# Second feed-forward of a two-block kernel: the up product of four slots in eight as seven block products, in 13 of 16 passes

## The chip, the cores and the metric

The kernel runs on one core of a Trainium2 chip. The metric is the device time of one execution in microseconds (us). Three executions of the kernel before took 2435.14, 2436.72 and 2437.55 us; the median is 2436.72 us.

## The reference, cut to what matters

Two transformer blocks of width 2048 run over 256 tokens in float32. The change lies in the last step of the second block, whose hidden width is 8192:

```
D_MODEL, SEQ = 2048, 256
D_FF_2 = 4 * D_MODEL

u = rms_norm_2(h, norm_mlp_w[l])
h = h + jnp.square(jax.nn.relu(u @ w_up[l])) @ w_down[l]
...
return rms_norm_2(h, norm_final_w)
```

## The kernel before, in words

All large products have one form. A **slot** is a piece of a weight matrix of 256 rows and 512 columns, 512 KB, held as [128, 2 x 512]. The chip's SyncE (SP) issues one DMA for each slot into one of four places of `raw` (`RING = 4`), ScalarE (ACT) rounds it to fp32r in `w_hi` (`split`, L904 to L910), VectorE (DVE) writes what is left over to `w_lo` = `raw` - `w_hi` (L1422 to L1426), and TensorE (PE) multiplies: for each of 2 token tiles and 2 row tiles three matmuls of 512 moving columns (`gemm`, L484 to L500: activation high x weight high, activation high x weight low, activation low x weight high), 12 in all. The activations are the stationary operand, so each matmul loads 128x128 of them.

The ring sets the order: the load of slot q starts when `w_lo` of slot q-4 is done (L401, L442, semaphore `w_lo_ready`); ACT splits slot q three slots ahead of PE, as soon as the load has landed and PE has done slot q-4 (`landed`, `slot_done`); DVE follows ACT (`w_hi_ready`); PE waits for `w_lo_ready`. Every engine works its queue in the written order.

The second feed-forward runs in 16 passes over chunks of 512 hidden columns. A pass i has 16 slots: 0 to 7 are the up product of chunk i over 2048 input rows (`ups2`; operands `B_hi`, `B_lo`; PSUM banks 0 and 1), 8 to 15 the down product of chunk i-1 into four column chunks of the result (`downs2`, operands `C_hi`, `C_lo`, banks `D2_BANKS`, two slots for each chunk), which DVE adds to `resid` (`add_chunk`, L1473). After slot 7 ACT takes the up product out of PSUM in four pieces with the rms scale and a relu (L933), DVE squares it (L1923) and transposes it in 32x32 blocks (L1926), and GpSimd (POOL) sends it to DRAM and back in four DMAs (`turn_rows`, L2131 and L2135), which completes the transposition. In the next pass ACT and DVE split what came back into `C_hi` and `C_lo` (`up2_operand`, L1348 and L1909, behind the split of slot 5). POOL does nothing else in this stage.

## Time and profile before

| | |
|---|---|
| median of three executions | 2436.72 us |
| the profiled execution, span | 2435.7 us |
| PE matmul busy | 2409.6 us, 99% |
| DVE busy | 1642.3 us, 67% |
| ACT busy | 1285.9 us, 53% |
| POOL busy | 215.8 us, 9% |
| one pass of the second feed-forward | 41.4 us |

The span is the time from the first to the last instruction on the core; about 1 us lies around it. A matmul's record lasts from its issue to its modelled end, so records overlap: the pace of PE is the distance between two starts, not the mean of a record. A line number can be that of a helper that serves the whole kernel (L496 to L498 are all of the matmuls of `gemm`).

### The profile page before, as it was taken

What the parts mean: (1) busy time and instruction counts of PE and PEld (TensorE: products, weight loads), DVE (VectorE), ACT (ScalarE), POOL (GpSimd) and SP (SyncE); (2) the same over time, 40 slices, a digit from 0 to 9 for tenths busy, and PEclk for the clock granted to TensorE, in tenths of its full rate; (3) what the DMA queues carried; (4) which work ended last, traced back from release to release, by engine and by line L of the source; (5) the groups of instructions that cost most, each with busy time, mean ns of one, the idle gap of its engine ahead of it and who ended that gap; (6) DMA issues with size and microseconds to landing.
All of it is one profiled execution on the core that took longest, in us unless ns stands there. A gap on an engine that the chain in (4) does not pass through costs nothing. (4 is left out here: it accounts for less than half of the span.)

```text
span 2435.7 us, 32600 instructions
## 1 busy us (share of the span) xinstructions
PE 2409.6 (99%) x11468; PEld 2111.4 (87%) x11468; DVE 1642.3 (67%) x1831; ACT 1285.9 (53%) x1715; POOL 215.8 (9%) x364
## 2 busy tenths in 40 slices
PE   8999999999999999999999999999999999999997
PEld 7888888888888888888889888888888888888886
DVE  5666665777777777776877655566666666666666
ACT  6555555655555555564444555555554444444444
POOL 0111101100000000000010100000110000000000
PEclk9999999999999999999999999999999999999999
DMA  7877777887787778767566866578877877777775
GB/s 233 274 216 225 216 218 233 248 239 234 240 236 238 235 234 237 221 195 227 179 200 189 245 193 209 178 226 252 250 235 216 235 224 230 227 231 226 224 232 161
DMA packets 270391, 545.79 MB, mean 224 GB/s; under 512 B 22011, under 2 KB 23395, under 8 KB 270179
## 3 DMA queue, kind: packets, MB, share of 16 engines
q1 hardware_dynamic: 244064, 469.82, 63.4%
q0 software_dynamic: 22192, 70.28, 10.4%
q10 hardware_dynamic: 4051, 4.59, 0.6%
q8 instruction: 50, 0.82, 0.1%
q14 instruction: 34, 0.28, 0.0%
HBM read 508.93 MB, written 35.68 MB: 224 GB/s over the span
## 5 line engine op out<-in xcount | busy, mean ns | idle before, releaser
L1426 DVE TENSOR_TENSOR w_lo<-raw,w_hi 128x1024 fp32r<-128x1024 f32 x887 | 1078.9, 1222 | 661.6 <-ACT w_hi L910 656.5
L910 ACT ACTIVATE w_hi<-raw 128x1024 fp32r<-128x1024 f32 x887 | 934.3, 1056 | 919.0 <-PE acc L498 785.1
L496 PE MATMUL acc<-w_hi,A_hi 128*128 128x512 f32 x1932 | 741.2, 384 | 2.2 <-DVE A_lo L1909 1.7
L498 PE MATMUL acc<-w_hi,A_lo 128*128 128x512 f32 x1932 | 733.2, 379 | 0.0
L497 PE MATMUL acc<-w_lo,A_hi 128*128 128x512 f32 x1932 | 733.1, 379 | 0.0
L496 PEld LDWEIGHTS acc<-w_hi,A_hi 128*128 128x128 f32 x1932 | 366.0, 189 | 55.2 <-issue 2.9
L498 PEld LDWEIGHTS acc<-w_hi,A_lo 128*128 128x128 f32 x1932 | 365.9, 189 | 51.0
L497 PEld LDWEIGHTS acc<-w_lo,A_hi 128*128 128x128 f32 x1932 | 366.2, 190 | 49.3
L496 PE MATMUL acc<-w_hi,B_hi 128*128 128x512 f32 x800 | 304.9, 381 | 0.6 <-DVE B_lo L1693 0.6
L496 PE MATMUL acc<-w_hi,C_hi 128*128 128x512 f32 x800 | 303.7, 380 | 0.0
L497 PE MATMUL acc<-w_lo,B_hi 128*128 128x512 f32 x800 | 303.6, 379 | 0.0
L498 PE MATMUL acc<-w_hi,C_lo 128*128 128x512 f32 x800 | 303.6, 379 | 0.0
L497 PE MATMUL acc<-w_lo,C_hi 128*128 128x512 f32 x800 | 303.5, 379 | 0.0
L498 PE MATMUL acc<-w_hi,B_lo 128*128 128x512 f32 x800 | 303.5, 379 | 0.0
L496 PEld LDWEIGHTS acc<-w_hi,B_hi 128*128 128x128 f32 x800 | 151.6, 189 | 22.0 <-DVE B_lo L1693 1.0
L496 PEld LDWEIGHTS acc<-w_hi,C_hi 128*128 128x128 f32 x800 | 151.5, 189 | 21.3 <-DVE w_lo L1426 0.2
L498 PEld LDWEIGHTS acc<-w_hi,B_lo 128*128 128x128 f32 x800 | 151.5, 189 | 21.2
L498 PEld LDWEIGHTS acc<-w_hi,C_lo 128*128 128x128 f32 x800 | 151.5, 189 | 21.2
L497 PEld LDWEIGHTS acc<-w_lo,C_hi 128*128 128x128 f32 x800 | 151.5, 189 | 21.1
L497 PEld LDWEIGHTS acc<-w_lo,B_hi 128*128 128x128 f32 x800 | 151.5, 189 | 20.9
L1473 DVE TENSOR_TENSOR resid<-resid,acc 128x1024 f32<-128x1024 f32 x114 | 138.7, 1217 | 9.5 <-PE acc L498 9.0
L933 ACT ACTIVATE scratch<-acc,small 128x256 f32<-128x256 f32 x196 | 77.1, 473 | 64.4 <-PE acc L498 64.4
(208 smaller groups left out, 1296.5 us busy)
## 6 DMA issues: line engine op xcount, KB each, us to landing
raw<-in_up SPq DMA_DIRECT2D x304, 512.0 KB, 4.5
raw<-in_w SPq DMA_DIRECT2D x271, 512.0 KB, 4.4
raw<-in_down SPq DMA_DIRECT2D x216, 512.0 KB, 4.9
raw<-in_wo SPq DMA_DIRECT2D x64, 512.0 KB, 4.9
turn_rows<-scratch POOLq DMA_DIRECT2D x23, 512.0 KB, 3.2
scratch<-turn_rows POOLq DMA_DIRECT2D x92, 128.0 KB, 5.8
up_rows<-scratch POOLq DMA_DIRECT2D x21, 512.0 KB, 5.2
scratch<-up_rows POOLq DMA_DIRECT2D x84, 128.0 KB, 5.1
```

The source lines that it names most:

```text
L496: pe.matmul(o, hi[:, kt, ts], wh, start=first and kk == 0, stop=False)
L497: pe.matmul(o, hi[:, kt, ts], wl, start=False, stop=False)
L498: m = pe.matmul(o, lo[:, kt, ts], wh, start=False, stop=last and kk == SLOT_K - 1)
L910: act.activation(w_hi[:, q % RING, :], raw[:, q % RING, :], ACT.Copy).then_inc(w_hi_ready, 1)
L933: m = act.activation(by_block(dst, t)[:, h * JT // 2:(h + 1) * JT // 2], src, func, scale=scale[:, t:t + 1])
L1426: dve.tensor_tensor(w_lo[:, q % RING, :], raw[:, q % RING, :], f32(w_hi[:, q % RING, :]), ALU.subtract).then_inc(w_lo_ready, 1)
L1473: dve.tensor_tensor(v, v, acc[:, banks[0]:banks[1] + 1, :].rearrange("p t (n h) -> p t h n", h=2), ALU.add).then_inc(done, 1)
```

## The change

In passes 2 to 14 (13 passes) the up slots 1, 3, 5 and 7 are multiplied by Strassen's scheme in Winograd's form. A slot's product is seen as a 2x2 block product (two token tiles by two row tiles, times two row tiles by two halves of 256 columns) and takes seven block products of 256 columns, each as three matmuls, so 21 matmuls of 256 columns (`gemm_by_seven`). Four of the seven use sums of weight blocks. POOL makes them from `raw` in three instructions per slot (`make_sums`, two chained waits between them), and ACT and DVE split these sums in addition to 768 of the slot's own 1024 columns. The sums go into free room of `A_hi` and `A_lo`. Four sums of activation blocks for all four slots are made once, ahead of pass 2 (`make_forms` on POOL, ACT and DVE). The other up slots of these passes keep their 12 matmuls of 512 columns, but with the columns in another order (`gemm_by_halves`: each half of 256 for itself).

The seven products gather in PSUM banks 0 to 3. Behind slot 7 ACT copies banks 2 and 3 to SBUF, DVE combines them in three small instructions and adds banks 0 and 1 to the result (`quarters`); ACT applies the relu to it in four pieces and then squares it, which DVE did before. These relu and square stand behind two down slots (`q == 1`), the transposition on DVE behind three (`q == 2`), and `up2_operand` stands behind the split of slot 7 instead of slot 5. The down product uses banks 4 to 7 in turn in place of six banks and waits for the additions of the chunk two before.

```diff
-        D2_BANKS, D2_LAST = [BK[1], BK[2], BK[3], BK[1]], [BK[0], BK[2], BK[3], BK[1]]
+        D2_BANKS, D2_LAST = [BK[2], BK[3], BK[2], BK[3]], [BK[0], BK[2], BK[3], BK[1]]
...
+        Q = CW // 2
+        SEVEN = (1, 3, 5, 7)
+        SEVEN_FROM, SEVEN_TO = 2, FFN2 - 1
...
+            def gemm_by_halves(R, p, hi, lo, kp, banks, first):
+
+                pe.wait_ge(w_lo_ready, RING * R + p + 1)
+                ring = p % RING
+                for t in range(TT):
+                    for kk in range(SLOT_K):
+                        kt = kp * SLOT_K + kk
+                        wh, wl = (half_in_turn(w[:, ring, kk * CW:(kk + 1) * CW]) for w in (w_hi, w_lo))
+                        o, ts = half_columns(acc[:, banks[t], :]), slice(t * P, (t + 1) * P)
+                        pe.matmul(o, hi[:, kt, ts], wh, start=first and kk == 0, stop=False)
+                        pe.matmul(o, hi[:, kt, ts], wl, start=False, stop=False)
+                        m = pe.matmul(o, lo[:, kt, ts], wh, start=False, stop=False)
...
+                for bank, half, act_pair, w_pair, starts, stops in (
+                        (x0, 1, of_token(1, 0), of_slot(3), False, False),
+                        (x0, 0, of_form(3), of_slot(2), False, True),
+                        (c1, 1, of_token(0, 0), of_slot(1), True, False),
+                        (x1, 1, of_token(1, 1), of_sum(3), False, True),
+                        (c0, 0, of_form(0), of_sum(0), True, False),
+                        (c1, 0, of_form(1), of_sum(2), False, True),
+                        (c0, 1, of_form(2), of_sum(1), False, True)):
+                    o = columns(acc[:, bank, half * Q:(half + 1) * Q])
+                    wh, wl = (in_turn(w) for w in w_pair)
+                    pe.matmul(o, act_pair[0], wh, start=first and starts, stop=False)
+                    pe.matmul(o, act_pair[0], wl, start=False, stop=False)
+                    m = pe.matmul(o, act_pair[1], wh, start=False, stop=last and stops)
+                m.then_inc(slot_done, 1)
...
             def downs2(R, p0, i, operand, banks=D2_BANKS):
-                downs(R, p0, banks, [None, None, None, (down2_out, 4 * i - 3)], (up2_lo, i), None, operand)
+                downs(R, p0, banks, [None, (up2_out, i), (down2_out, 4 * i - 3), (down2_out, 4 * i - 2)], (up2_lo, i), None, operand)
...
-            pe.wait_ge(down2_out, 3)
-            with pe.Fori(2, FFN2) as i:
+            pe.wait_ge(forms_lo, 1)
+            with pe.Fori(SEVEN_FROM, SEVEN_TO) as i:
                 R = R7 + U2 + B7 * (i - 1)
-                ups2(R, i)
+                ups2_by_seven(R, i)
                 downs2(R, SPC, i, (C_hi, C_lo))
-                pe.wait_ge(down2_out, 4 * i - 1)
...
+            def split_by_seven(R, q, i, p):
+
+                act.wait_ge(landed[q % RING], 16 * (R + q // RING + 1))
+                act.wait_ge(slot_done, RING * R + q - AHEAD)
+                act.activation(w_hi[:, q % RING, Q:], raw[:, q % RING, Q:], ACT.Copy).then_inc(part_hi, 1)
+                act.wait_ge(sums_made, nth_seven(i, p) + 1)
+                act.activation(sums_of(A_hi, p), sums32[:, SEVEN.index(p) % 2, :], ACT.Copy).then_inc(w_hi_ready, 1)
...
+            def pass2(R, i, following=True):
+
+                for p in range(SPC):
+                    split2(R, p, i, True, following)
+                    if p == 4:
+                        act.wait_ge(slot_done, RING * R)
+                        up2_operand(i - 1, C_hi)
+                act.wait_ge(slot_done, RING * R + SPC)
+                act.wait_ge(quarters_made, i - SEVEN_FROM)
+                act.activation(corner(0, 4), acc[:, 2:4, :].rearrange("p b c -> p (b c)"), ACT.Copy).then_inc(corner_kept, 1)
...
+                dve.wait_ge(part_hi, nth_seven(i, p) + 1)
+                dve.tensor_tensor(w_lo[:, q % RING, Q:], raw[:, q % RING, Q:], f32(w_hi[:, q % RING, Q:]), ALU.subtract)
+                dve.wait_ge(w_hi_ready, RING * R + q + 1)
+                dve.tensor_tensor(sums_of(A_lo, p), sums32[:, SEVEN.index(p) % 2, :], f32(sums_of(A_hi, p)),
+                                  ALU.subtract).then_inc(w_lo_ready, 1)
...
+            def make_sums(i, p):
+
+                ring, n = p % RING, nth_seven(i, p)
+                pool.wait_ge(landed[ring], 16 * (R7 + U2 + B7 * (i - 1) + p // RING + 1))
+                src, dst = raw[:, ring, :], sums32[:, SEVEN.index(p) % 2, :]
+                chain.link(pool.tensor_tensor(dst[:, 0:2 * Q].rearrange("p (a n) -> p a n", a=2),
+                                              src[:, Q:3 * Q].rearrange("p (a n) -> p a n", a=2),
+                                              src[:, 0:Q].unsqueeze(1).to_broadcast([P, 2, Q]), ALU.subtract))
+                chain.link(pool.tensor_tensor(dst[:, 2 * Q:3 * Q], dst[:, Q:2 * Q], src[:, Q:2 * Q], ALU.add))
+                pool.tensor_tensor(dst[:, 3 * Q:4 * Q], src[:, 3 * Q:4 * Q], dst[:, 2 * Q:3 * Q],
+                                   ALU.subtract).then_inc(sums_made, 1)
...
                 pool.dma_start(turn_rows, block_x).then_inc(up2_sent, 16)
+                following = [p for p in SEVEN if by_seven(i + 1, p)]
+                for p in following[:1]:
+                    make_sums(i + 1, p)
                 pool.wait_ge(up2_sent, 16 * (i + 1))
                 pool.wait_ge(*((up2_lo, i) if i else (turn_dve, TN_RES2 + 3)))
                 for b in range(4):
                     pool.dma_start(block_t[32 * b:32 * (b + 1), :].rearrange("p (a e) -> p a e", a=4),
                                    rows_by_quad[b]).then_inc(up2_back, 16)
+                for p in following[1:]:
+                    make_sums(i + 1, p)
```

POOL's queue in the middle of the stage. Before, it holds for each pass the send to `turn_rows` and the four DMAs back:

```order
L2131 DMA turn_rows<-scratch 128x1024 [waits up2_back,up2_block]
L2135 DMA scratch<-turn_rows 32x4x256 [waits up2_lo,up2_sent]
L2135 DMA scratch<-turn_rows 32x4x256 x3
L2131 DMA turn_rows<-scratch 128x1024 [waits up2_back,up2_block]
L2135 DMA scratch<-turn_rows 32x4x256 [waits up2_lo,up2_sent]
L2135 DMA scratch<-turn_rows 32x4x256 x3
```

After the change, from one send on (TENSOR_TENSOR rows are `make_sums`; `landed1` and `landed3` are the loads of slots 1 and 3, then 5 and 7):

```order
L2366 DMA turn_rows<-scratch 128x1024 [waits up2_back,up2_block]
L2351 TENSOR_TENSOR scratch<-raw 128x512 [waits landed1]
L2354 TENSOR_TENSOR scratch<-scratch,raw 128x256 [waits pool_self]
L2355 TENSOR_TENSOR scratch<-raw,scratch 128x256 [waits pool_self]
L2373 DMA scratch<-turn_rows 32x4x256 [waits up2_lo,up2_sent]
L2373 DMA scratch<-turn_rows 32x4x256 x3
L2351 TENSOR_TENSOR scratch<-raw 128x512 [waits landed3]
L2354 TENSOR_TENSOR scratch<-scratch,raw 128x256 [waits pool_self]
L2355 TENSOR_TENSOR scratch<-raw,scratch 128x256 [waits pool_self]
L2351 TENSOR_TENSOR scratch<-raw 128x512 [waits landed1]
L2354 TENSOR_TENSOR scratch<-scratch,raw 128x256 [waits pool_self]
L2355 TENSOR_TENSOR scratch<-raw,scratch 128x256 [waits pool_self]
```

The sums of the next pass's slot 1 stand between the send and the return; twelve instructions with SBUF inputs are new in each pass.

DVE's queue in the pass, from the split of slot 8 to the first addition to `resid`. Before (the rows that only compute the loop's wait values left out):

```order
L1426 TENSOR_TENSOR w_lo<-raw,w_hi 128x1024 [waits w_hi_ready]
...
L1426 TENSOR_TENSOR w_lo<-raw,w_hi 128x1024 [waits w_hi_ready]
...
L1923 TENSOR_TENSOR scratch<-scratch 128x1024 [waits up2_out]
...
L1926 STREAM_TRANSPOSE scratch<-scratch 128x1024 [waits up2_sent]
...
L1426 TENSOR_TENSOR w_lo<-raw,w_hi 128x1024 [waits w_hi_ready]
...
L1426 TENSOR_TENSOR w_lo<-raw,w_hi 128x1024 [waits w_hi_ready]
L1473 TENSOR_TENSOR resid<-resid,acc 128x2x512 [waits slot_done]
```

After:

```order
L1575 TENSOR_TENSOR w_lo<-raw,w_hi 128x1024 [waits w_hi_ready]
L2109 TENSOR_TENSOR scratch<-scratch 128x256 [waits corner_kept]
...
L2111 TENSOR_TENSOR scratch<-scratch 128x256 [waits corner_sum]
...
L2113 TENSOR_TENSOR scratch<-scratch 128x2x256 [waits corner_sum]
...
L2118 TENSOR_TENSOR scratch<-acc,scratch 128x1024 [waits up2_out,corner_sum]
...
L1575 TENSOR_TENSOR w_lo<-raw,w_hi 128x1024 [waits w_hi_ready]
...
L1575 TENSOR_TENSOR w_lo<-raw,w_hi 128x1024 [waits w_hi_ready]
L1622 TENSOR_TENSOR resid<-resid,acc 128x2x512 [waits slot_done]
...
L1575 TENSOR_TENSOR w_lo<-raw,w_hi 128x1024 [waits w_hi_ready]
...
L2125 STREAM_TRANSPOSE scratch<-scratch 128x1024 [waits up2_sent]
```

Four instructions of the combination stand ahead of `w_lo` of slot 11, and the transposition comes one addition later, behind `w_lo` of slot 13.

## Rows read from the trace of the kernel before

**Rows 1.** The page: busy time and count of an engine; TensorE's granted clock.

```profile
PE 2409.6 (99%) x11468; PEld 2111.4 (87%) x11468; DVE 1642.3 (67%) x1831; ACT 1285.9 (53%) x1715; POOL 215.8 (9%) x364
...
PEclk9999999999999999999999999999999999999999
```

**Rows 2.** PE's longest waits in the whole span: us in total, times, longest.

```profile
PE acc L555 <- DMA scratch<-in_rows: 5.8, 1, 5.8
PE acc L621 <- DVE scratch L1493: 1.8, 1, 1.8
```

**Rows 3.** Busy time in two stretches that make one pass, and their sum.

```profile
2007.50:2030.80 23.30, 23.30 (x110) 20.44 (x109) 17.09 (x15) 10.97 (x13) 2.74 (x5) 1.00 0.83 231
2030.80:2048.90 18.10, 18.10 (x86) 15.88 (x85) 10.36 (x9) 8.35 (x8) 0.00 (x0) 1.00 0.72 220
sum 41.40, PE 41.40 PEld 36.31 DVE 27.45 ACT 19.32 POOL 2.74; mean PE 20.70 PEld 18.16 DVE 13.72 ACT 9.66 POOL 1.37
```

**Rows 4.** PE in order of time: start, duration; matmuls of 512 columns, twelve apart.

```profile
2030.72 0.38 PE L496 MATMUL acc<-w_hi,B_hi 128*128 128x512 f32 x1
...
2033.31 0.38 PE L496 MATMUL acc<-w_hi,B_hi 128*128 128x512 f32 x1
```

**Rows 5.** PE in order of time: plain f32 matmuls of 256 and 128 columns.

```profile
1381.96 0.59 PE L791 MATMUL acc<-pT,scratch 128*128 128x256 f32 x2
1382.40 0.38 PE L792 MATMUL acc<-pT,scratch 128*128 128x128 f32 x2
1382.62 0.49 PE L621 MATMUL acc<-const,scratch 128*128 128x128 f32 x3
```

**Rows 6.** PE in order of time: fp32r matmuls of 256 columns, weights 32 columns.

```profile
39.03 0.28 PE L580 MATMUL acc<-A_lo,C_hi 128*32 128x256 f32 x1
39.15 0.28 PE L579 MATMUL acc<-A_hi,C_hi 128*32 128x256 f32 x1
39.26 0.28 PE L580 MATMUL acc<-A_lo,C_hi 128*32 128x256 f32 x1
```

**Rows 7.** Groups of instructions on ACT and DVE: count, busy us, mean ns.

```profile
L1426 DVE TENSOR_TENSOR w_lo<-raw,w_hi 128x1024 fp32r<-128x1024 f32 x887 | 1078.9, 1222 | 661.6 <-ACT w_hi L910 656.5
L910 ACT ACTIVATE w_hi<-raw 128x1024 fp32r<-128x1024 f32 x887 | 934.3, 1056 | 919.0 <-PE acc L498 785.1
```

**Rows 8.** DVE instructions of 256 and 512 columns: duration ns min/median/max.

```profile
L1498 DVE TENSOR_TENSOR B_lo<-acc,B_hi x24: 410/418/425, 112.9 to 1552.7; 128x256 fp32r<-128x256 f32 x24
L1768 DVE TENSOR_TENSOR scratch<-scratch x16: 684/686/936, 1142.6 to 1321.6; 128x512 f32<-128x512 f32 x16
```

**Rows 9.** Groups of instructions on POOL: count, busy us, mean ns.

```profile
L2035 POOL CAST levels<-scratch 128x1024 uint8<-128x1024 f32 x1 | 1.1, 1106 | 0.0
L1999 POOL TENSOR_TENSOR small<-small 128x2 f32<-128x2 f32 x4 | 0.8, 191 | 136.7 <-DVE small L1467 136.7
```

**Rows 10.** DVE and POOL in order of time, around POOL's only instruction with 1024 input columns.

```profile
72.79 3.16 DVE L1426 TENSOR_TENSOR w_lo<-raw,w_hi 128x1024 fp32r<-128x1024 f32 x2
...
73.76 1.11 POOL L2035 CAST levels<-scratch 128x1024 uint8<-128x1024 f32 x1
```

**Rows 11.** DVE and POOL in order of time, around a POOL instruction of 8 columns.

```profile
53.39 1.21 DVE L1426 TENSOR_TENSOR w_lo<-raw,w_hi 128x1024 fp32r<-128x1024 f32 x1
...
53.55 1.11 POOL L1999 TENSOR_TENSOR small<-small 128x8 f32<-128x8 f32 x1 [17.22 <-DVE small L1576]
```

**Rows 12.** ACT and DVE in order of time, slot 7 to 13; x2 is two instructions.

```profile
2007.61 1.57 ACT L933 ACTIVATE scratch<-acc,small 128x256 f32<-128x256 f32 x4 [1.53 <-PE acc L498]
2009.05 2.20 ACT L910 ACTIVATE w_hi<-raw 128x1024 fp32r<-128x1024 f32 x2
...
2010.56 1.25 DVE L1926 STREAM_TRANSPOSE scratch<-scratch 128x1024 f32<-128x1024 f32 x1
2011.73 2.32 DVE L1426 TENSOR_TENSOR w_lo<-raw,w_hi 128x1024 fp32r<-128x1024 f32 x2
```

**Rows 13.** DMA issues at 2012.7, at 2016.4 and 2029.2 us: median us to landing.

```profile
raw<-in_down SPq DMA_DIRECT2D x1, 512.0 KB, 4.8
...
raw<-in_up SPq DMA_DIRECT2D x1, 512.0 KB, 8.7
...
raw<-in_up SPq DMA_DIRECT2D x1, 512.0 KB, 4.5
```

**Rows 14.** All 98 loads of up slots from 1850 to 2350 us.

```profile
DMA to landing us min/median/max: 3.6/6.0/9.2
```

**Rows 15.** ACT in order of time: splits of slots 1 and 4 of a pass.

```profile
2025.33 1.06 ACT L910 ACTIVATE w_hi<-raw 128x1024 fp32r<-128x1024 f32 x1 [3.71 <-DMA raw<-in_up]
...
2030.92 1.06 ACT L910 ACTIVATE w_hi<-raw 128x1024 fp32r<-128x1024 f32 x1 [1.53 <-PE acc L498]
```

More of the change, by code:

```diff
@@ new lines, in gemm_by_seven, with of_token, of_form, of_slot @@
+            def gemm_by_seven(R, p, hi, lo, first, last):
+                pe.wait_ge(w_lo_ready, RING * R + p + 1)
+                s, ring = SEVEN.index(p), p % RING
+                whole_hi, whole_lo = (w[:, SLOT_K * p:SLOT_K * (p + 1), :] for w in (hi, lo))
+                form_hi, form_lo = forms_of(A_hi), forms_of(A_lo)
+                def of_token(k, t):
+                    return whole_hi[:, k, t * P:(t + 1) * P], whole_lo[:, k, t * P:(t + 1) * P]
+                def of_form(f):
+                    return form_hi[:, f, s, :], form_lo[:, f, s, :]
+                def of_slot(k):
+                    return tuple(w[:, ring, k * Q:(k + 1) * Q] for w in (w_hi, w_lo))
+                def of_sum(k):
+                    return tuple(sums_of(w, p)[:, k * Q:(k + 1) * Q] for w in (A_hi, A_lo))
+                x0, x1 = BK[0]
+                c0, c1 = BK[1]
+                for bank, half, act_pair, w_pair, starts, stops in (
[11 more added lines that the diff above has]
+                    m = pe.matmul(o, act_pair[1], wh, start=False, stop=last and stops)
+                m.then_inc(slot_done, 1)
@@ L876, in last_downs @@
+            downs2(R_END - 2 - B7, SPC, FFN2 - 1, (C_hi, C_lo))
             def last_downs():
@@ L1371, in _ @@
             for q in range(2 * NCH):
-                split(R7 + U2, SPC + q)
-            with act.Fori(2, FFN2 - 1) as i:
-                R = R7 + U2 + B7 * (i - 1)
-                ups2(R, i)
-                for q in range(2 * NCH):
-                    split(R, SPC + q)
-            ups2(R_END - 2 - B7, FFN2 - 1)
+                split2(R7 + U2, SPC + q, 1, False, True)
+                if q == 2:
+                    make_forms()
+            with act.Fori(SEVEN_FROM, SEVEN_TO - 1) as i:
+                pass2(R7 + U2 + B7 * (i - 1), i)
+            pass2(R7 + U2 + B7 * (SEVEN_TO - 2), SEVEN_TO - 1, following=False)
+            ups2(R_END - 2 - B7, FFN2 - 1, at=4)
             for q in range(2 * NCH):
```

128 lines of the change are left out of this document (121 added, 7 removed).

## The prediction

> **What bounds the kernel now.** I read the page first: PE has matmuls in flight for 99% of the span at full granted clock (2.4 GHz), DVE is busy 67%, ACT 53%, POOL 9% [rows 1]. PE's waits come next, and the reader should see how little there is: the longest is 5.8 us at the start, the next 1.8 us [rows 2]. One pass of the stage takes 41.4 us, with PE busy in all of it, DVE 27.45, ACT 19.32, POOL 2.74 [rows 3]. So this stage is bound by PE's own pace: twelve matmuls of 512 columns, a slot, from 2030.72 to 2033.31, 2.59 us [rows 4]; sixteen slots give 41.4. Only fewer or shorter matmuls help, and only while the other engines deliver a slot's weights within that pace.
>
> Last I looked for the slack of the delivery. The up loads land 3.6 to 9.2 us after issue, median 6.0 [rows 14], since the return from `turn_rows` shares the DMA engines with them: one issued while it runs takes 8.7 us, one issued later 4.5 [rows 13]. ACT then waits 3.71 us for the load of slot 1; at slot 4 it is ahead again and waits for PE [rows 15]. PE never notices. But the ring is already tight there, and the change puts a third engine into it.
>
> **PE's part.** A slot by seven has 21 matmuls of 256 columns, each with a fresh load of 128x128 weights. No row shows exactly that, so I bound it. Plain f32 takes two cycles for a column: 256 columns take 0.44/2 = 0.22 us, 128 columns 0.22/2 = 0.11 us, with a full weight load behind each [rows 5]. An fp32r matmul of 256 columns has as many cycles as the latter. The fp32r matmuls of 256 columns in the trace start 0.12 us apart (39.03 to 39.26 is 0.23 for two), with small weights [rows 6]. That gives 21 x 0.11 = 2.3 to 21 x 0.117 = 2.46 us for a slot; I take 2.3, as the full load fits behind 0.11 and the column order is interleaved as in the 512-column matmuls. Four slots of 13 passes save 52 x 0.13 = 7 to 52 x 0.29 = 15 us; a pass has 40.3 us of PE work by the lower price, 40.9 by the higher. The other four up slots keep their count; I see no reason for them to slow, and the bound is the pace of the 256s, 0.23 for 512 columns instead of 0.216 (12 x 52 x 0.018 = 11 us).
>
> **ACT and DVE.** A 1024-column instruction costs 1.06 us on ACT and 1.22 on DVE [rows 7], one of 256 0.42, of 512 0.69 on DVE [rows 8]. ACT gets four pieces of 768 (0.8 each), the copy (1.1) and the square (1.06) more: 19.3 + 5.4 = 24.7 us of a pass. DVE gets four of 768 (0.95 each), and 0.42 + 0.42 + 0.69 + 1.22, and loses the square (1.22): 27.5 + 5.3 = 32.8. Both are below 40.3. The banks hold too: the addition that releases banks 4 and 5 has 5.2 us (two slots) for 1.2 us of work. In sum of busy time nothing but PE binds.
>
> **POOL's part.** Its only instruction over 1024 elements with SBUF input, the cast, takes 1.11 us, and a tensor_tensor of two columns 0.19 [rows 9]. With two inputs I take twice the cast's rate: 2.2 us for the 1024 columns of a slot's sums, plus three starts of 0.17, 2.7 us; if both inputs were read at once it would be 1.6, and the upper bound is 4, for strides and broadcasts that no row has. The Trainium skill, GPSIMD Engine Reference, "Performance versus the Vector engine", gives 4.5 us for a two-input add of 2048 columns, by an estimate 2.25 for 1024; by it the sum would stay.
>
> What decides is that POOL and DVE shut each other out. While the cast ran (73.76 to 74.87) the second of two `w_lo` instructions should have ended at 72.79 + 2.32 = 75.11 [rows 10, 12], but ended at 75.95, which is the cast's end and 1.08 us of work: it stood still for the cast's whole rest. The other way round, a POOL instruction of 8 columns that met `w_lo` at 53.39 took 1.11 us and ended with it, where 0.2 is usual [rows 9, 11]. Who asked first goes first. The Trainium skill, SBUF — State Buffer, "Who interferes with whom", states it as an exclusive lock for a DVE instruction with two SBUF inputs against a GpSimd one that reads SBUF; the additions and the transposition on DVE are free of it by that page. By it alone the sum would be the one below, so its only use is to say that these rows are no accident.
>
> **The circle.** Slot 5's load waits for `w_lo` of slot 1, and slot 1's for slot 13 of the pass before. I follow it once round, each step beginning where the one before ends:
> 1. `w_lo` of 13 to `w_lo` of 1: issue 0.2, landing 5.2 (4.8 before the return, [rows 13]; the return now stands behind the sums), sums 2.7, DVE's turns between them 1.0, ACT 1.06 and DVE 1.22: 11.4 us.
> 2. `w_lo` of 1 to `w_lo` of 5: issue 0.2, landing 7, since the return's four DMAs are issued right behind the sums of slot 1 (4.5 to 8.7, [rows 13]), sums 2.7, DVE in between 2.2 (two of its instructions, one before and one between), ACT and DVE 2.3: 14.4.
> 3. Slot 7's sums follow slot 5's on POOL: 2.7 + 2.2 = 4.9, with the same 2.3 behind.
> 4. PE's slot 7 and its handoff: 2.5. ACT's copy 1.1; DVE's combination, 0.42 + 0.42 + 0.69 + 1.22 and its waits 2.9, behind a `w_lo` on hand 0.5; relu 1.6 [rows 12], behind a split 0.5; square 1.2; slot 13's split 1.06 + 1.22: 12.6 in all.
>
> The sum is 43.3 us, more than PE's 40.3. PE then waits for `w_lo` in the up slots, some 3 us in each pass, and a pass takes 43.3 - 41.4 = 1.9 us longer than before, 13 x 1.9 = 25 us. The single preparation (POOL about 9 us, ACT and DVE 2 each) is covered by 20 us of the first up part; if not, it costs up to 3. The profiled execution took 2435.7 and 1.0 lies around it, so 2436.7, the median's 2436.72: 2436.7 + 25 = **2461.5 us**. With DVE before each of nine POOL instructions (9 x 1.2 instead of 5.4) a pass takes 48.7; with sums at 1.6 us and half the blocking 37, so PE binds.
>
> **The rivals.** (a) **PE stays the bound**: the circle stays under 40.3 because POOL fits into DVE's gaps (40.3 - 32.8 = 7.5 us of a pass) or adds faster. Then 2436.7 less 7 to 15 is 2422 to 2430 us, faster. For it: DVE has that idle time, the sum for each engine is below 40.3, and the blocking of 5.4 us is the least certain term; without it the circle has 37.9. Against it: DVE's gaps are waits for ACT, and at slots 1 to 7 it is the ring that is late, not PE. It decides at 41.4 us: the circle may lose 1.9 us of 43.3 before the sign turns. (b) **The two cancel**, a circle of 41.0 to 41.8, or faster products with slower 512s: 2432 to 2441. (c) **DVE comes first every time** or the sums cost 4 us: 47 to 48.7 us a pass, 2510 to 2531. (d) **The change doesn't do what it says**: if a 256-column matmul can't go below its weight load, and took the 0.216 of a 512 one, a slot would cost 4.5 us, 52 x 1.95 = 101 us more; the 128-column rows at 0.11 speak against it.
>
> **How the numbers follow.** The forecast, a circle above PE's work with 2442 to 2500 us as its own range, 0.59; (a) 0.25; (b) 0.09; (c) 0.06; (d) 0.01. Leaving out (c), (d) and the upper end of the forecast, the range is 2422 to 2495. Faster or slower counts from 0.2%, 5 us, about what a measurement of this kernel can tell from no change: faster 0.26, within it 0.09, slower 0.65.
>
> **What would show it.** Right: the three `make_sums` groups mean 1.2 and 0.65 us or more, with the excess of those that met DVE; `w_lo` instructions of over 2 us; PE waits behind DVE's `w_lo` in up slots of each pass, first at slot 3 or 5; 256-column matmuls 0.11 apart; passes of 43 us with 40.3 us of PE work. Wrong: no PE waits in the loop (rival a), starts 0.12 apart or more, or waits at slots 12 and 14, which would be the banks that I took as safe.

## The result, and the profile after

The changed kernel takes 2448.31 us (median of four executions, 2446.55 to 2450.96) against 2436.93 us (2435.14 to 2437.55) of the kernel before beside it: 1.0045 times as long, 95% interval 1.0031 to 1.0059, 11.4 us more. The prediction said 25 us more. The sign and the range (2422 to 2495) held, the size was more than twice too large. A second measurement gave 2451.08 against 2439.13 us, ratio 1.0051 (1.0038 to 1.0065).

The page of the changed kernel, busy time and count of each engine and TensorE's granted clock, to be held beside [rows 1]:

```profile
PE 2402.3 (98%) x11936; PEld 2109.1 (86%) x11936; DVE 1776.9 (73%) x1923; ACT 1352.4 (55%) x1794; POOL 448.8 (18%) x525
...
PEclk9999999999999999999999999999999999999999
```

PE has 468 matmuls more and is busy 7 us less, DVE has gained 135 us and POOL 233. The clock is not in it: in this execution it is at its full 2.4 GHz through the whole stage. In some of the variants below it is not. PE's longest waits come next (us in total, times, longest), against [rows 2]:

```profile
PE acc L948 <- DVE A_lo L2088: 16.0, 17, 1.4
PE acc L596 <- DMA scratch<-in_rows: 5.2, 1, 5.2
PE acc L537 <- DVE C_lo L2058: 2.9, 1, 2.9
PE acc L537 <- DVE w_lo L1575: 1.5, 2, 1.0
```

The first row is the loop: the first matmul of a slot by seven (L948) waits for the low half of that slot's sums (L2088). The third row is new too and happens once, as pass 1 begins its down product. Three matmuls of a slot by seven, and ahead of them the end of such a wait (start, duration):

```profile
2082.56 0.38 PE L948 MATMUL acc<-w_hi,B_hi 128*128 128x256 f32 x1 [0.81 <-DVE A_lo L2088]
...
2082.89 0.28 PE L950 MATMUL acc<-w_hi,B_lo 128*128 128x256 f32 x1
2083.00 0.28 PE L948 MATMUL acc<-w_hi,A_hi 128*128 128x256 f32 x1
2083.11 0.28 PE L949 MATMUL acc<-w_lo,A_hi 128*128 128x256 f32 x1
```

They start 0.11 us apart (0.1117 over all of them), 21 to a slot are 2.345 us where twelve of 512 columns took 2.59 [rows 4]. PE's work fell by 52 x 0.244 = 12.7 us, and more than that came back as waiting.

A table from the starts of PE's matmuls in the profiled executions shows where. "First" is the up part of pass 0, counted from its ninth matmul on, and the whole of pass 1, where the preparation lies; "thirteen" is passes 2 to 14; "rest" is all behind them.

| kernel | first, us | thirteen, us | rest, us | one of the thirteen |
|---|---|---|---|---|
| before | 19.9 + 41.4 | 538.7 | 76.1 | 41.4 |
| changed | 21.1 + 44.6 | 547.3 | 75.1 | 41.3 to 42.9 |
| changed, second measurement | 21.1 + 42.4 | 546.4 | 75.4 | 40.6 to 42.8 |

The thirteen passes lose 8.6 us: 12.7 saved, 21.3 of waiting ahead of slots 3, 5 and 7 (3.7, 7.4 and 8.3 us, the rest behind them). The preparation costs 4.4 us, 2.2 in the second measurement. What lies ahead moved the other way in this execution (the ninth matmul stands at 1756.6 us, before at 1759.6). That part varies without any edit: by 2.0 us between the two profiled executions of the changed kernel, and by up to 5.7 us over all the variants, whose code is the same up to there. So where a variant is judged by a few us, the table of its stage says more than its total.

What stretched on POOL and DVE (count, busy us, mean ns, idle before):

```profile
L2351 POOL TENSOR_TENSOR scratch<-raw 128x512 f32<-128x512 f32 x52 | 80.6, 1551 | 63.0 <-DMA raw<-in_up 62.9
L2354 POOL TENSOR_TENSOR scratch<-scratch,raw 128x256 f32<-128x256 f32 x52 | 82.1, 1580 | 4.1
L2355 POOL TENSOR_TENSOR scratch<-raw,scratch 128x256 f32<-128x256 f32 x52 | 56.1, 1079 | 4.1
L2086 DVE TENSOR_TENSOR w_lo<-raw,w_hi 128x768 fp32r<-128x768 f32 x52 | 69.2, 1330 | 0.9 <-ACT w_hi L1480 0.9
L2088 DVE TENSOR_TENSOR A_lo<-scratch,A_hi 128x1024 fp32r<-128x1024 f32 x52 | 70.0, 1347 | 36.5 <-ACT A_hi L1482 36.5
L1575 DVE TENSOR_TENSOR w_lo<-raw,w_hi 128x1024 fp32r<-128x1024 f32 x835 | 1065.1, 1285 | 528.7 <-ACT w_hi L1011 524.3
```

The three sums of a slot take 1.55 + 1.58 + 1.08 = 4.21 us. The two instructions of 256 columns do the same amount of work and differ by 0.5 us: the first of them nearly always meets a DVE instruction that got in during the hand-over.

One round of the circle, on POOL, from slot 1's sums (the first three) to slot 7's:

```profile
2069.14 1.66 POOL L2351 TENSOR_TENSOR scratch<-raw 128x512 f32<-128x512 f32 x1 [1.99 <-DMA raw<-in_up]
2070.87 1.59 POOL L2354 TENSOR_TENSOR scratch<-scratch,raw 128x256 f32<-128x256 f32 x1
2072.54 0.73 POOL L2355 TENSOR_TENSOR scratch<-raw,scratch 128x256 f32<-128x256 f32 x1
2073.22 2.22 POOL L2373 DMA_DIRECT2D scratch<-turn_rows  x4
2075.45 1.31 POOL L2351 TENSOR_TENSOR scratch<-raw 128x512 f32<-128x512 f32 x1
...
2080.14 1.29 POOL L2351 TENSOR_TENSOR scratch<-raw 128x512 f32<-128x512 f32 x1 [0.89 <-DMA raw<-in_up]
2081.51 1.59 POOL L2354 TENSOR_TENSOR scratch<-scratch,raw 128x256 f32<-128x256 f32 x1
2083.17 1.59 POOL L2355 TENSOR_TENSOR scratch<-raw,scratch 128x256 f32<-128x256 f32 x1
2086.50 1.75 POOL L2351 TENSOR_TENSOR scratch<-raw 128x512 f32<-128x512 f32 x1 [1.73 <-DMA raw<-in_up]
```

And on DVE, the low halves of slots 13, 1, 5 and 7, with which the prediction's steps end, and of slot 13 of the next round:

```profile
2063.91 1.23 DVE L1575 TENSOR_TENSOR w_lo<-raw,w_hi 128x1024 fp32r<-128x1024 f32 x1 [1.72 <-ACT w_hi L1011]
...
2074.40 1.23 DVE L2088 TENSOR_TENSOR A_lo<-scratch,A_hi 128x1024 fp32r<-128x1024 f32 x1 [0.31 <-ACT A_hi L1482]
2075.54 2.31 DVE L1575 TENSOR_TENSOR w_lo<-raw,w_hi 128x1024 fp32r<-128x1024 f32 x1
...
2085.89 1.23 DVE L2088 TENSOR_TENSOR A_lo<-scratch,A_hi 128x1024 fp32r<-128x1024 f32 x1 [0.31 <-ACT A_hi L1482]
...
2092.45 1.22 DVE L2088 TENSOR_TENSOR A_lo<-scratch,A_hi 128x1024 fp32r<-128x1024 f32 x1 [1.71 <-ACT A_hi L1482]
...
2106.19 1.23 DVE L1575 TENSOR_TENSOR w_lo<-raw,w_hi 128x1024 fp32r<-128x1024 f32 x1 [1.79 <-ACT w_hi L1011]
```

Their ends are 2065.14, 2075.63, 2087.12, 2093.67 and 2107.42: steps of 10.5, 11.5, 6.55 and 13.75 us, 42.3 in all, where the prediction had 11.4, 14.4, 4.9 and 12.6, 43.3 in all. Slot 2's low half (2075.54) stands still for 1.1 of its 2.31 us beside slot 3's first sum on POOL (2075.45).

### The profile page after: what moved, and what is told of

Read it like the earlier page. It is cut to its first block and busy times, and to the rows that moved or that the text cites. A ratio compares the mean times of both kernels' runs of the same rounds, so it can differ in the third digit from the quotient of the medians.

```text
span 2444.8 us, 34010 instructions
## 1 busy us (share of the span) xinstructions
PE 2402.3 (98%) x11936; PEld 2109.1 (86%) x11936; DVE 1776.9 (73%) x1923; ACT 1352.4 (55%) x1794; POOL 448.8 (18%) x525
## 5 line engine op out<-in xcount | busy, mean ns | idle before, releaser
L1575 DVE TENSOR_TENSOR w_lo<-raw,w_hi 128x1024 fp32r<-128x1024 f32 x835 | 1065.1, 1285 | 528.7 <-ACT w_hi L1011 524.3
L1011 ACT ACTIVATE w_hi<-raw 128x1024 fp32r<-128x1024 f32 x835 | 873.7, 1054 | 701.0 <-PE acc L539 598.1
L538 PEld LDWEIGHTS acc<-w_lo,C_hi 128*128 128x128 f32 x800 | 151.2, 189 | 21.1
L537 PE MATMUL acc<-w_hi,B_hi 128*128 128x512 f32 x384 | 147.0, 383 | 1.6 <-DVE w_lo L1575 1.0
L538 PE MATMUL acc<-w_lo,B_hi 128*128 128x512 f32 x384 | 145.5, 379 | 0.0
L539 PE MATMUL acc<-w_hi,B_lo 128*128 128x512 f32 x384 | 145.5, 379 | 0.0
L1482 ACT ACTIVATE A_hi<-scratch 128x1024 fp32r<-128x1024 f32 x52 | 55.1, 1059 | 155.3 <-POOL scratch L2355 155.3
L1622 DVE TENSOR_TENSOR resid<-resid,acc 128x1024 f32<-128x1024 f32 x114 | 138.2, 1212 | 2.0 <-PE acc L539 1.7
L2088 DVE TENSOR_TENSOR A_lo<-scratch,A_hi 128x1024 fp32r<-128x1024 f32 x52 | 70.0, 1347 | 36.5 <-ACT A_hi L1482 36.5
L2277 POOL DMA_DIRECT2D up_rows<-scratch x21 | 11.8, 562 | 459.1 <-DVE scratch L1804 459.1
L2351 POOL TENSOR_TENSOR scratch<-raw 128x512 f32<-128x512 f32 x52 | 80.6, 1551 | 63.0 <-DMA raw<-in_up 62.9
```

The source lines that it names most:

```text
L537: pe.matmul(o, hi[:, kt, ts], wh, start=first and kk == 0, stop=False)
L538: pe.matmul(o, hi[:, kt, ts], wl, start=False, stop=False)
L539: m = pe.matmul(o, lo[:, kt, ts], wh, start=False, stop=last and kk == SLOT_K - 1)
L1011: act.activation(w_hi[:, q % RING, :], raw[:, q % RING, :], ACT.Copy).then_inc(w_hi_ready, 1)
L1482: act.activation(sums_of(A_hi, p), sums32[:, SEVEN.index(p) % 2, :], ACT.Copy).then_inc(w_hi_ready, 1)
L1575: dve.tensor_tensor(w_lo[:, q % RING, :], raw[:, q % RING, :], f32(w_hi[:, q % RING, :]), ALU.subtract).then_inc(w_lo_ready, 1)
```

## The experiments

My theory: POOL's reads and DVE's instructions with two SBUF inputs shut each other out, and this stretching, added to POOL's own work, makes the ring's circle longer than PE's work, in the preparation as in the loop. The rivals: the length of the chain by itself, without any blocking; DVE's added work; the return DMAs, which lengthen the loads. The experiments lie on three chips; each ratio is to the kernel before on the same chip.

**POOL writes, but reads nothing** (three memsets of 1024 columns instead of three sums; the variant leaves the true weight sums out, so its result is not the product):

```diff
-                chain.link(pool.tensor_tensor(dst[:, 0:2 * Q]..., src[:, Q:3 * Q]..., src[:, 0:Q]..., ALU.subtract))
-                chain.link(pool.tensor_tensor(dst[:, 2 * Q:3 * Q], dst[:, Q:2 * Q], src[:, Q:2 * Q], ALU.add))
-                pool.tensor_tensor(dst[:, 3 * Q:4 * Q], src[:, 3 * Q:4 * Q], dst[:, 2 * Q:3 * Q],
-                                   ALU.subtract).then_inc(sums_made, 1)
+                chain.link(pool.memset(dst, 1.0))
+                chain.link(pool.memset(dst, 1.0))
+                pool.memset(dst, 1.0).then_inc(sums_made, 1)
```

> The changed kernel, with each slot's three sum instructions on POOL replaced by three memsets of the same 1024-column destination (the true weight sums are left out, so the seven products use constants in their place). POOL is then busy for about the same 2.8 us a slot (1.28 + 0.73 + 0.73 us are the shortest instances of the sums), behind the same wait for the load, but reads nothing from SBUF. Theory 1, POOL and DVE shut each other out: the sums no longer take 3.8 to 4.8 us from start to end but 2.8, DVE's w_lo is 1.2 us throughout, and nearly all of the 21 us of PE waits in front of the slots by seven go: 2448.3 - 21 = 2427 to 2431 us. Theory 2, it is the length of the chain itself (load, 2.8 us on POOL, ACT, DVE, next load) that is too long for the ring, blocked or not: the waits stay, 2443 to 2448 us. A value between says how it is shared.

Measured: 2426.09 us, ratio 0.9957 (0.9941 to 0.9974). The thirteen passes took 526.0 us, each exactly 40.5, which is PE's work; not one wait was left in them. The groups of this run:

```profile
L2351 POOL MEMSET scratch<- 128x1024 f32 x52 | 49.9, 959 | 80.4 <-DMA raw<-in_up 80.3
L2086 DVE TENSOR_TENSOR w_lo<-raw,w_hi 128x768 fp32r<-128x768 f32 x52 | 49.6, 955 | 16.8 <-ACT w_hi L1480 16.7
L2088 DVE TENSOR_TENSOR A_lo<-scratch,A_hi 128x1024 fp32r<-128x1024 f32 x52 | 63.7, 1224 | 22.4 <-ACT A_hi L1482 21.8
```

POOL spends 0.96 us on each of three, 2.9 us a slot, a little more than the 2.74 that undisturbed sums take, in the same place of the same chain. So it is neither the chain's own length nor the work that ACT, DVE and the return DMAs have more, all of which stayed. What is missing is the stretching: 768 columns take 0.955 us instead of 1.33, the sums' low half 1.22 instead of 1.35. The prediction's sum without blocking was 37.9 us for the circle, under PE's 40.3, and this run bears out that it lies under PE's work. The first part stayed at 21.1 + 43.7 us, since the preparation still reads.

**The sums on DVE** (and the preparation's long addition in four pieces):

```diff
+                dve.wait_ge(landed[q % RING], 16 * (R + q // RING + 1))
+                dve.tensor_tensor(dst[:, 0:2 * Q]..., src[:, Q:3 * Q]..., src[:, 0:Q]..., ALU.subtract).then_inc(sum_step, 1)
+                dve.wait_ge(sum_step, 2 * n + 1)
+                dve.tensor_tensor(dst[:, 2 * Q:3 * Q], dst[:, Q:2 * Q], src[:, Q:2 * Q], ALU.add).then_inc(sum_step, 1)
+                dve.wait_ge(sum_step, 2 * n + 2)
+                dve.tensor_tensor(dst[:, 3 * Q:4 * Q], src[:, 3 * Q:4 * Q], dst[:, 2 * Q:3 * Q],
+                                  ALU.subtract).then_inc(sums_made, 1)
                 dve.wait_ge(part_hi, nth_seven(i, p) + 1)
```

> The three sum instructions of each slot are on DVE, ahead of its 768-column part, instead of on POOL (preparation in four pieces). DVE gets 0.69 + 0.42 + 0.42 = 1.5 us a slot more, 6.1 a pass, on top of 1776.9 us busy: about 33 + 6 = 39 us of a pass of 40.3, but no instruction of POOL is in its way. Theory 1, the cost was the blocking between the two engines: PE waits less than with POOL, 2430 to 2440 us. Theory 2, the cost is simply DVE's and the ring's load: DVE at 39 of 40.3 us has no slack, waits grow, 2450 to 2470 us.

Measured: 2433.15 us, ratio 0.9982 (0.9971 to 0.9992), faster than the kernel before by 4.3 us. Two groups of the profile after, the 512-column sum and the 768 columns:

```profile
L2088 DVE TENSOR_TENSOR scratch<-raw 128x512 f32<-128x512 f32 x52 | 35.6, 685 | 0.0
...
L2097 DVE TENSOR_TENSOR w_lo<-raw,w_hi 128x768 fp32r<-128x768 f32 x52 | 49.5, 952 | 0.0
```

The three sums cost DVE 0.685 + 0.425 + 0.425 = 1.54 us a slot, yet its busy time over the whole kernel is 1778.7 us, as with the sums on POOL (1776.9): the standing still had cost as much as the work itself. In both kernels DVE is as full, but its time is now spent in one piece: the thirteen passes take 531.0 us instead of 547.3, with some 5 us of waiting left out of 21. The first part took 19.9 + 46.0 us, 1.7 us of it by 3.4 us at half the clock. DVE is at 275 of 300 us (1900 to 2200 us); that this sets what is left is borne out by the version with three slots below, whose loop has no wait.

**Two slots of a pass instead of four** (3 and 7):

```diff
-        SEVEN = (1, 3, 5, 7)
+        SEVEN = (3, 7)
```

(The preparation's long addition is cut in four pieces here too, as in the variant after this one.)

> Only slots 3 and 7 of a pass go by seven products (1 and 5 by halves as the other four), the preparation's long addition in four pieces. The saving on PE is half, 26 x 0.244 = 6.3 us. Theory 1, the ring falls behind because the sums of slots 1, 3, 5, 7 follow one another with POOL and DVE in each other's way: with every fourth slot by seven there are two slots of ordinary delivery between them, the PE waits in the loop go, and 2436.9 - 6.3 + 1 to 3 of preparation gives 2431 to 2434 us. Theory 2, every slot by seven is late by itself: 2436.9 - 6.3 + 21/2 + 2 = 2443 us.

Measured: 2437.89 us, ratio 0.9997 (0.9988 to 1.0007), a miss of 4 us by the number. In the loop the first theory holds exactly: thirteen passes of 40.9 to 41.0 us, 532.3 in all, which is 538.7 - 6.4, and no wait. What I had wrong is the preparation, put at 1 to 3 us: the first part took 19.9 + 47.9, 6.5 us more than before, and the rest 78.2 instead of 76.1. That is the longest of this variant's ten executions (2442.36 us), so these two figures are at the high end. A part of them is TensorE's clock: behind PE's wait for `C_lo` (3.35 us) the granted clock was 0.50, 1.2 GHz, for 6.8 us, and behind a wait near the end for 3.4 us more. Together these stretches cost some 4.5 us, and the changed kernel's profile has none of this in the stage.

**The preparation's long addition in pieces**:

```diff
-                pool.tensor_tensor(whole, ks(B_hi), ks(B_lo), ALU.add).then_inc(whole_made, 1)
-                pool.wait_ge(whole_made, 1)
+                for s in range(len(SEVEN_FORMS)):
+                    pool.tensor_tensor(whole[:, s], ks(B_hi)[:, s], ks(B_lo)[:, s], ALU.add).then_inc(whole_made, 1)
+                pool.wait_ge(whole_made, len(SEVEN_FORMS))
```

> The changed kernel with one edit: POOL's one addition of 2048 columns in the preparation is cut into four of 512. In the trace of the changed kernel a w_lo of 4.49 us stands beside it, followed by a PE wait of 1.5 us, and PE waits 2.9 us for C_lo where pass 2 begins. Theory 1, these waits come from DVE standing still for the whole long instruction: in four pieces w_lo gets its turn between them, and the kernel is 1 to 4 us faster than the changed one, 2444 to 2447 us. Theory 2, the preparation's cost is the order of its steps on ACT and DVE: no difference, 2448 us.

Measured: 2453.27 us, ratio 1.0061 (1.0043 to 1.008). The gain of the first theory did not come. By the ratio this is not told from the changed kernel either (1.0045 and 1.0051 in its two measurements); what can be read is the stage. POOL in this run:

```profile
1771.29 7.95 POOL L2337 TENSOR_TENSOR scratch<-B_hi,B_lo 128x512 f32<-128x512 f32 x4
...
1785.98 2.31 POOL L2346 TENSOR_TENSOR scratch<-scratch 128x512 f32<-128x512 f32 x1
1788.24 0.60 POOL L2368 DMA_DIRECT2D turn_rows<-scratch  x1
```

The pieces let DVE in (the up part of pass 0 is back at 19.9 us), but DVE's turns make POOL's addition 7.95 us long where it was 4.55 in one piece. So the activation sums end at 1788.24, later than the block that POOL should send was ready: the send follows without any idle time, `C_lo` comes late (PE waits 3.9 us), and pass 1 takes 47.3 us, 1.7 us of it by 3.4 us at half the clock behind that wait.

**The preparation behind the first return**:

```diff
-                if i == 0:
-                    make_forms()
                 pool.wait_ge(up2_block, i + 1)
...
                     pool.dma_start(block_t[32 * b:32 * (b + 1), :]...).then_inc(up2_back, 16)
+                if i == 0:
+                    make_forms()
```

(ACT and DVE split these sums one down slot later.)

> The changed kernel with the preparation moved: POOL makes the four activation sums behind the first return instead of ahead of the first send, and ACT and DVE split them one slot later. In the trace of the changed kernel the first up part and pass 1 take 21.1 + 44.6 us instead of 19.9 + 41.4 before (+4.4), with a PE wait of 2.9 us for C_lo. Theory 1, the preparation costs because it stands in POOL's queue and in DVE's way just ahead of the first send: 61.3 to 63 us for both, and 2448.3 - 2 to 4 = 2444 to 2446 us. Theory 2, it costs wherever it stands (ACT's and DVE's extra instructions): no difference.

Measured: 2455.52 us, ratio 1.0074 (1.0059 to 1.0089); the first part took 19.9 + 45.3 us, 1.7 us of it by 3.4 us at half the clock. No gain. DVE's queue in order of time shows why; in the kernel before, the same three `w_lo` take 1.23 us each:

```profile
1790.27 8.79 DVE L1575 TENSOR_TENSOR w_lo<-raw,w_hi 128x1024 fp32r<-128x1024 f32 x3 [1.36 <-ACT w_hi L1011]
1798.98 2.29 DVE L2058 TENSOR_TENSOR C_lo<-scratch,C_hi 128x1024 fp32r<-128x1024 f32 x1
```

Three `w_lo` take 8.79 us instead of 3.7, and `C_lo`, for which PE waits, begins 2.0 us after ACT's half is there (1796.94) and takes 2.29 us instead of 1.23. The send was on time here, so POOL's queue was not the reason in this run: the reads were. The loop, untouched by this edit, took 552.8 us (546.4 to 552.8 in all the runs with sums on POOL in the changed order); why the same loop varies by 6 us stays open.

**The preparation with writes only** (the variant leaves the activation sums out), and the changed kernel once more on the same chip:

```diff
-                pool.tensor_tensor(whole, ks(B_hi), ks(B_lo), ALU.add).then_inc(whole_made, 1)
+                chain.link(pool.memset(whole, 1.0))
+                pool.memset(whole, 1.0).then_inc(whole_made, 1)
...
-                pool.tensor_tensor(forms32[:, 0], a21, a22, ALU.add).then_inc(form_made, 1)
...
+                for f in range(4):
+                    for _ in range(3):
+                        chain.link(pool.memset(forms32[:, f], 1.0))
+                    pool.memset(forms32[:, f], 1.0).then_inc(form_made, 1)
```

> The changed kernel with the real sums of the weights on POOL in the loop, but the preparation's five additions replaced by memsets of about the same total time that read nothing (the activation sums are left out, so the seven products use constants in their place). Theory 1, the preparation's 4.4 us come from POOL's reads standing in DVE's way: the first up part and pass 1 take 61.3 to 62 us, as before the change, and the time is 3 to 4.4 us below the changed kernel beside it. Theory 2, they come from the instructions that ACT and DVE have more and from POOL's queue: 65 us as in the changed kernel, same time.

> The changed kernel itself, unaltered, on the chip of the runs beside it, since the runs so far were compared with its first measurement. 2448 us if the chips agree; 2450 to 2453 if what the runs with the preparation cut in pieces (2453) or moved (2455) showed lies in the chip and not in the edit.

Measured: 2447.11 us, ratio 1.0036 (1.0022 to 1.005). The changed kernel once more took 2451.08 us, ratio 1.0051 (1.0038 to 1.0065), between its first ratio (1.0045) and that of the preparation in pieces (1.0061), so no effect of the pieces on the total is shown. With writes only the first part took 19.9 + 41.4 us, to a tenth what it took before the change, in a profiled execution whose loop was no shorter (550.4 us). POOL's memsets occupied it for 12.6 us where the additions took 13.4, and ACT and DVE kept their instructions. So those are free and the reads cost all of it. (The intervals of the two totals overlap; what decides is the first part, 61.3 us here against 63.5 to 67.8 in the ten profiled executions in which POOL reads in the preparation, and still 63.5 at least where a stretch at half the clock is taken off.)

**The return ahead of slot 1's sums**:

```diff
                 pool.dma_start(turn_rows, block_x).then_inc(up2_sent, 16)
-                for p in following[:1]:
-                    make_sums(i + 1, p)
                 pool.wait_ge(up2_sent, 16 * (i + 1))
...
-                for p in following[1:]:
+                for p in following:
                     make_sums(i + 1, p)
```

> The changed kernel with POOL's order turned round: the four DMAs of the return are issued ahead of slot 1's sums, not behind them. It tests the landing term of the prediction. There the loads beside the return were put at 7 to 8.7 us; in the trace of the changed kernel the up loads land in a median of 4.1 us. Theory 1, the late return is what keeps the loads quick (the return then runs while the ring holds fewer loads, or at another time): with the return first slot 1's load lands 3 us later, the PE waits before slots 3, 5 and 7 grow from 1.6 to 3 or 4 us a pass, and the time is 2465 to 2490 us. Theory 2, the order has no part in it: within 5 us of 2448.

Measured: 2483.45 us, ratio 1.0193 (1.0177 to 1.0208). The number is that of the first theory, but not for its reason. The up loads landed in a median of 4.2 us, against 4.1 in the changed kernel. POOL in this run:

```profile
2081.50 0.56 POOL L2366 DMA_DIRECT2D turn_rows<-scratch  x1 [18.33 <-DVE scratch L2125]
2087.47 2.20 POOL L2371 DMA_DIRECT2D scratch<-turn_rows  x4 [5.41 <-DMA turn_rows<-scratch]
2089.69 1.29 POOL L2351 TENSOR_TENSOR scratch<-raw 128x512 f32<-128x512 f32 x1
2091.05 0.73 POOL L2354 TENSOR_TENSOR scratch<-scratch,raw 128x256 f32<-128x256 f32 x1
2091.86 0.72 POOL L2355 TENSOR_TENSOR scratch<-raw,scratch 128x256 f32<-128x256 f32 x1
```

POOL's queue waits 5.41 us for the send to land and 2.20 to issue the return, and only then begins slot 1's sums, for data that had been there: the price of a wait is what is queued behind it. PE now waits ahead of slot 1 (34.5 us over the loop), and the loop takes 582.9 us. Some 11 us of the 35.6 by which it grew are a second price, TensorE's clock. One such wait (PE, start and duration), and the granted clock of the stretch behind it (0.50 in the last row):

```profile
2094.99 0.58 PE L948 MATMUL acc<-w_hi,B_hi 128*128 128x256 f32 x1 [3.16 <-DVE A_lo L2088]
...
2095.78 0.42 PE L948 MATMUL acc<-w_hi,A_hi 128*128 128x256 f32 x1
2096.00 0.42 PE L949 MATMUL acc<-w_lo,A_hi 128*128 128x256 f32 x1
...
2096.00:2098.00 2.00, 2.00 (x11) 2.00 (x11) 2.00 (x3) 0.78 (x1) 1.19 (x1) 0.50 0.84 224
```

At 1.2 GHz the matmuls start 0.21 us apart instead of 0.11. Six of the twelve passes whose slot 1 came late have such a stretch, 23.9 us in all; the others, with waits of up to 3.15 us, have none. The last three rows of POOL above are also the only undisturbed set of sums in that stretch, since DVE itself stands idle there: 1.29 + 0.73 + 0.72 = 2.74 us.

**Versions that beat both.** With the sums on DVE I moved the preparation behind the first return, then took slot 3 out, then put the preparation on DVE too, in three down slots of pass 1 (`add_forms`, five instructions):

```diff
-        SEVEN = (1, 3, 5, 7)
+        SEVEN = (1, 5, 7)
...
                 split2(R7 + U2, SPC + q, 1, False, True)
+                add_forms(q)
```

> Sums on DVE as before, with the preparation behind the first return (as in the run beside it). With sums on DVE the thirteen passes took 531.0 us against 538.7 before, and the preparation 65.9 against 61.3. Theory 1 of the preparation: 2433 - 3 = 2429 to 2431 us. Theory 2: 2433 us.

> As the run before it, with three slots of eight by seven products (1, 5, 7; slot 3 by halves). PE's saving is 39 x 0.244 = 9.5 us instead of 12.7, but DVE has 3 us less in a pass. With four slots PE waited 5 us over the stage, mostly ahead of slot 3. If DVE's fill sets those waits they go, and the time is the same or 1 to 2 us lower: 2428 to 2430 us. If each slot by seven is late by itself, it is 2431 to 2434 us.

> Weight sums and activation sums both on DVE (the latter one after another behind the splits of the first three down slots of pass 1), POOL left with its DMAs; slots 1, 3, 5, 7. With the activation sums on POOL behind the first return this took 2433.3 us, the first up part and pass 1 63.5 us instead of 61.3, with three w_lo of DVE taking 8.3 us instead of 3.5 beside POOL. If POOL's reads were the reason: 61.3 to 62 us, and 2431 us. If DVE's own extra 5 us of work fill it: 64 us or more, 2433 to 2435.

> The same with slots 1, 5 and 7 by seven products. The thirteen passes took 529.2 us without one PE wait when only the weight sums were on DVE, the first up part and pass 1 65.2. By theory 1 of the run beside it 61.3 to 62 us there and 2431.1 - 3 = 2428 us; by the other 2431 us.

| sums, preparation, slots | time, us | before beside it | ratio (95%) | first | thirteen | rest |
|---|---|---|---|---|---|---|
| DVE, POOL later, 1 3 5 7 | 2433.26 | 2437.53 | 0.9979 (0.9970 to 0.9988) | 19.9 + 43.6 | 531.4 | 75.7 |
| DVE, POOL later, 1 5 7 | 2431.12 | 2437.53 | 0.9974 (0.9965 to 0.9984) | 19.9 + 45.3 | 529.2 | 78.1 |
| DVE, DVE, 1 3 5 7 | 2435.81 | 2439.13 | 0.9985 (0.9976 to 0.9994) | 19.9 + 42.4 | 533.9 | 78.7 |
| DVE, DVE, 1 5 7 | 2431.62 | 2439.13 | 0.9969 (0.9957 to 0.9981) | 19.9 + 42.4 | 531.2 | 75.7 |

All four beat both kernels, by 0.15 to 0.31% the kernel before. The second row's first part and rest and the third row's rest hold a stretch of 3.4 us at half the clock each, 1.7 us, behind a wait of PE of 1.9 to 2.6 us; without it the second row's first part is the first row's. The last has the lowest ratio, 7.5 us less than before, but its interval overlaps the others'. With three slots a pass takes 40.7 us, which is PE's work, without a wait; with four, PE's work would be 40.46, but DVE is too full and the pass takes about 40.9. Fewer fast slots give the same or less time. With the preparation on DVE `C_lo` is no longer late and the first part falls to 62.3 us, above the 61.3 to 62 that I had put there: DVE's 5 us of extra work show at slot 12 of pass 1, where PE waits 0.7 us for an addition to `resid` that frees its bank, and in pass 2 (42.7 us instead of 40.7; 43.8 with four slots), so most of the gain was handed on. The first version came out at its second theory's 2433 us, by the number, though its first part did fall (63.5 us from 65.9 with the preparation in pieces, of which 1.7 is a stretch at half the clock in the latter). The second is at the 2431 us of the rival, but its loop has no wait, as the first theory said. The third is nearer the second theory's 2433 to 2435 us. Against the expectation of 2428 us the last version is a miss of 3.6 us, of which the kernel before beside it explains some 1.6 (2439.1; 2437.5 on the chip of the first two rows).

## Why the prediction was right or wrong

**PE's part: right.** Predicted 2.3 us for a slot and 15 us saved, bounds 7 to 15; measured 2.345 and 12.7. The 512-column matmuls of the other up slots kept their pace. The Trainium skill, "TensorE: Matmul & The Clock Gate", "Back-to-back issue gap", gives N/2.4 + 2.5 ns for the gap of an isolated matmul; by an estimate from it that is 109 ns for 256 columns and 2.29 us for a slot. This trace, in a stream with weight loads, has 111.7 ns, 2 to 3% above it. For such a stream the page has about 131 ns for 512 columns, and there the trace differs: 216 ns [rows 4].

**ACT and DVE: right.** 32.8 us a pass predicted for DVE; in the loop where POOL reads nothing it was 239 of 300 us, 32.2 of a pass of 40.46; for ACT 24.7 predicted, and 185 of 300 us there, 25.0. In the changed kernel the banks never bound.

**POOL's sums: right by themselves.** 2.7 us predicted, 2.74 undisturbed.

**The blocking: right in kind and in size.** Predicted 1.0 + 2.2 + 2.2 us at three slots. Measured, the sums take 4.21 us on average, 1.47 more than undisturbed; in the round shown slot 1's 4.1 (3.7 predicted), slot 5's 4.6 (4.9), slot 7's 4.8 (4.9), together 5.4 us of blocking, as predicted. The run with writes only shows that this term alone carries the sign. It was called "the least certain term" there, and was the best.

**The circle: right as the bound, 1.2 us too long.** 43.3 predicted; 42.1 on average. The step that failed is the second, `w_lo` of 1 to `w_lo` of 5, and in it the landing: "landing 7, since the return's four DMAs are issued right behind the sums of slot 1". Slot 5's load took 4.3 us; issue and landing together 4.5 instead of 7.2. The 8.7 us of [rows 13] and the median 6.0 of [rows 14] come from a timing in which the return ran beside several loads; with the passes' new timing the up loads take 4.1 in the median and the return 3.8 per DMA instead of 6.6, while the send takes 5.2 instead of 3.2. I carried a duration from one timing of the transfers into another one. In the round of [rows 13] 3.1 loads on average were in flight beside the return, by their issues and landings; in the round shown above 1.3. That the number of loads is the reason is argued and not shown: where POOL only writes, the loop keeps PE's pace and the up loads take 4.7 us. And it is not the order of return and sums: with the return first they took 4.2. Step 1 was too long in the same term (4.0 us of issue and landing instead of 5.4).

The third step failed the other way, 6.55 instead of 4.9: POOL was free for slot 7 at 2084.76 but waited 1.73 us for its load, whose ring place comes free with slot 3's low half. I had followed slots 1 and 5 only, as if slot 7 hung on POOL alone. The fourth was 13.75 instead of 12.6: the four relu took 2.20 us instead of 1.6, and ACT was behind a split that waited for its load. The three errors, -3.8, +1.65 and +1.15, leave -1.0 us of 43.3. In the sum over thirteen passes that is 25 predicted and 8.6 measured: a difference of two nearly equal numbers, 43.3 and 41.4, takes a 3% error of the first as a 65% error of itself. It is luck that the total, 11.4 us, came nearer to 25 than the loop did: the preparation, put at nothing, added its 4.4 us on the forecast's side.

**The preparation: wrong.** Put at nothing, up to 3 us, "covered by 20 us of the first up part". It cost 4.4 (2.2 in the second measurement, up to 6.5 in variants, of which some 3 us there are the clock). I looked at the idle time of the engines and did not see that POOL's reads stand in DVE's way there as in the loop, though I had just used that for the loop. DVE at the long addition:

```profile
L1575 DVE TENSOR_TENSOR w_lo<-raw,w_hi x4: 2291/2298/4487, 1767.8 to 1776.7; 128x1024 fp32r<-128x1024 f32 x4
```

One `w_lo` of 4.49 us (min/median/max here) stood beside a POOL addition of 4.55; PE lost 1.2 us there, and the chain behind carried the delay into `C_lo`. The chain grew on its way: from the issue of the first send to ACT's half of `C_lo` it took 15.2 us, before 13.2, so the transfers to DRAM and back took 2.0 us longer as well. With writes only both are back (13.3 us).

**The rivals.** (a) needed the circle under PE's work; for the sign to turn it had to lose 1.9 us of 43.3, and it lost 1.2. (b) needed the loop to end even, within 5 us; it ended 8.6 us up. (c), DVE first each time, did not occur. (d) fell with the first rows.

## What to carry to other kernels

Where GpSimd is handed work because it idles, look first at what DVE does in that time: if DVE runs instructions with two SBUF inputs and GpSimd reads SBUF, the work is paid on both engines, and here moving it to the busier DVE cost DVE nothing (1778.7 against 1776.9 us busy) and gained 16 us in the loop. A circle of handoffs decides by its difference to the bound, the time PE needs; price every step of it from rows with the same timing, and apply a mechanism that you have found to each place where it fits, the one-time parts too. A gain that is smaller but leaves the feeding engine slack (three slots of eight) can be worth as much as the larger one.
